# Inside one half-page step, VectorE's own product and sum go ahead of its sum of GpSimd's product

## The chip, the cores and the metric

The kernel runs on one core of a Trainium2 chip. The metric is the time of one launch on the device, in microseconds (us). Lower is better. The kernel before takes 874.13 us, the median of three runs (874.12 to 875.32).

## The reference

The reference is one inference step of a one-layer decoder trunk for 512 prompt tokens and 8 sample sequences (one new token each, 2048 past tokens in a paged cache). The part that matters here is the compression of the paged cache of the sample sequences. For each of the 8 sequences the cached rows are cut into segments of 16 tokens, and each segment is summed with two sets of 16 position weights. A compressed block is the first sum of one segment plus the second sum of the next:

```
def compress(rows, wpos, w, b):
    B, Tp = rows.shape[:2]
    seg = rows.reshape(B, Tp // CMP_STRIDE, CMP_STRIDE, NSA_KV_HEADS, HEAD_DIM)
    pooled = (jnp.einsum('bnjhd,jd->bnhd', seg[:, :-1], wpos[:CMP_STRIDE])
              + jnp.einsum('bnjhd,jd->bnhd', seg[:, 1:], wpos[CMP_STRIDE:]))
    return jnp.einsum('bnhd,de->bnhe', pooled, w) + b
```

Around it lie an input projection (`h @ w_in`), three kinds of attention, a matrix-memory recurrence, an output projection and a feed-forward network. Everything is float32.

## The kernel before

The values of the cache are compressed on VectorE and GpSimd; the keys are scored by TensorE straight from the pages. A sequence has 16 pages, loaded in two halves of 8 pages. There are 16 halves, numbered 0 to 15 here; half h belongs to sequence h // 2 and lives in one of two page buffers, h % 2. So "even" halves use one buffer and "odd" halves the other.

For each half h the engines do this:

- SyncE (`load_half`, L464) waits until the buffer is free: `comp_done` of half h - 2, and `slc_scored` of half h - 2 by TensorE. Then it issues 8 page loads (L471). Between two halves it issues one load of a weight slot (L455), which waits for GpSimd's `lo_ready`.
- GpSimd (`value_products`, L602) waits for the pages, and for `vmul_used` of half h - 1, and writes the product of the pages with the first 16 weights into the one scratch tile `tmpv`. Directly behind it stands the split of a weight slot (L622, the low part of a weight), which the projection on TensorE needs (`lo_ready`).
- VectorE (`half_sums`, L1474 on) waits for `vmul_ready`, sums `tmpv` over 16 (L1479, releases `tmpv` by `vmul_used`), multiplies the pages in place with the other 16 weights (L1482), and sums that (L1483, frees the page buffer by `comp_done`).
- After an odd half VectorE adds the two sums (L1630), and then, for sequences 1, 3, 4, 5 and 6, does one further piece of work for another branch: `gate_rows` (L1514 to L1518), `prompt_sums` (L1508, L1509, twice each), `gate_sums` (L1523 to L1525), `prompt_sums` again, and `gate_maxima` (L1529 to L1533). The last releases `rows_ready`, for which ScalarE waits before it evacuates the projection's item 17 (L1188).
- TensorE does one item of the projection (48 matmuls, L656) per half, between the scores of the pages (L740, L747). The item that stands behind half h needs the slot that GpSimd splits behind half h's product.

All engines run their instructions in the order of the program; nothing reorders them. The order is written out by hand.

Of the kernel before, what the change touches and what calls it, by code (L numbers as in the profile page):

```python
# [16 lines left out]
ALU = mybir.AluOpType  # L17
ACT = mybir.ActivationFunctionType
AX = mybir.AxisListType.X
# [148 lines left out]
def trunk_kernel(nc, xT, wst, par_d, con_d, hot_d, ltri_d, pt_d, cacheA, cacheV, winK, winV, mC, mst, plst, ffst,  # L168
                 o_y, o_fm, o_vn, o_st, o_snv, o_wk, o_wv, o_C, o_m, o_pool, o_sC, o_sn, o_sm, o_spool, o_ffp, o_ffs):
    with ExitStack() as ctx:  # L170
# [3 lines left out]
        def sem(name):  # L174
            return ctx.enter_context(nc.semaphore(name))
# [46 lines left out]
        def lay(at, parts):  # L222

            out = []
            for n in parts:
                out.append(arena[:, at:at + n])
                at += n
            return out


        qw, poolA, poolB, scs, _, sst = lay(0, [17 * P - 112, P, P, 2 * P, 256, 1024])
        scs = scs.rearrange("p (a n) -> p a n", a=2)
        poolA = poolA.rearrange("p (k n) -> p k n", k=2)
# [5 lines left out]
        tmpv = cst  # L239
# [90 lines left out]
        def par_(name, a=0, b=None, lo=0, hi=P):  # L330
            at, n = PAR[name]
            return par[lo:hi, at + a:at + (n if b is None else b)]
# [21 lines left out]
        vmul_ready, vmul_used = sem("vmul_ready"), sem("vmul_used")  # L354
# [1076 lines left out]
        def _(dve):  # L1431
            V = nc.vector
            chain = [0]

            def link(ins):

                chain[0] += 1
                ins.then_inc(dve_step, 1)
                dve.wait_ge(dve_step, chain[0])
# [34 lines left out]
            def half_sums(h):  # L1474


                b, s = h // 2, h % 2
                dve.wait_ge(vmul_ready, h + 1)
                V.tensor_reduce(poolA.rearrange("p k n -> p (k n)")[:, 64 * s:64 * s + 64], tmpv.rearrange("p (n j) -> p n j", j=16),  # L1479
                                AX, ALU.add).then_inc(vmul_used, 1)  # L1480
                v = pages[:, s, :, 2 * P:3 * P].rearrange("p a (n j) -> p a n j", j=16)
                link(V.tensor_tensor(v, v, par_("wpos", 48, 64).unsqueeze(1).unsqueeze(1).broadcast_to([P, HALF, 8, 16]), ALU.mult))  # L1482
                V.tensor_reduce(poolB.rearrange("p k n -> p (k n)")[:, 64 * s:64 * s + 64].rearrange("p (a n) -> p a n", a=HALF), v,  # L1483
                                AX, ALU.add).then_inc(comp_done, 1)
                dve.wait_ge(comp_done, h + 1)
                dve.wait_ge(vmul_used, h + 1)

# [127 lines left out]
            for c in range(1, 4):  # L1615
                group_mod(c)
                group_normed(c)
                if c == 2:
                    low(2)
            dve.wait_ge(rest_landed, 48)  # L1620
            half_sums(0)


            sample_query()
            for b in range(NB):
                for h in range(2 * b + (b == 0), 2 * b + 2):
                    half_sums(h)
                if b >= 2:
                    dve.wait_ge(blocks_done, b - 1)
                V.tensor_tensor(pooled[:, b % 2, 0:NCB], poolA.rearrange("p k n -> p (k n)")[:, 0:NCB],  # L1630
                                poolB.rearrange("p k n -> p (k n)")[:, 1:NCB + 1], ALU.add).then_inc(pooled_ready, 1)
                dve.wait_ge(pooled_ready, b + 1)
                if b == 1:
                    gate_rows()
                elif b == 3:
                    prompt_sums(0)
                elif b == 4:
                    gate_sums()
                elif b == 5:
                    prompt_sums(1)  # L1640
                elif b == 6:
                    gate_maxima()
# [373 lines left out]
            for m, (kind, t, _) in enumerate(PART2):  # L2016
# [15 lines left out]
                elif kind == "up":  # L2032
                    j, b = t % FC, t // FC
# [188 lines left out]
```

## Time and profile before

| what | us |
|---|---|
| median of three runs | 874.13 |
| the profiled execution, its own time | 879.95 |
| its span, first to last instruction | 877.3 |
| TensorE busy | 795.0 (91%) |
| VectorE busy | 499.2 (57%) |
| ScalarE busy | 328.9 (37%) |
| GpSimd busy | 297.0 (34%) |
| L602, GpSimd's product, 16 of them | 34.5 |
| L1479, VectorE's sum of it, 16 of them | 19.5 |
| L1482, VectorE's own product, 16 of them | 33.2 |

The profiled execution took 5.8 us more than the median of the runs. Its span is cut in 40 slices on the page; the halves fill slices 3 to 9 (46 to 206 us). Busy shares say little here: what counts is which wait ends last in that stretch.

### The profile page before, as it was taken

To read this page: it belongs to the slowest core of one execution; us is meant where nothing else is said; L and a number is where in the kernel's file an instruction comes from. 1 tells how busy PE (TensorE), PEld (TensorE's weight loads), DVE (VectorE), ACT (ScalarE), POOL (GpSimd) and SP (SyncE) were. 2 spreads that over 40 slices of the span, in tenths; PEclk is the share of its full clock that TensorE was granted. 3 is DMA by queue.
4 is the path that set the end of the run, shared out by engine and by line. 5 is a ranking of instruction groups with operands and counts; after the bars stand their busy time and mean duration, and the time that the engine had idled before them with its cause. 6 is when DMAs were issued, how large, how long until landed. Compare 5 with 4: busy or idle time off the path is not lost.

```text
span 877.3 us, 18760 instructions
## 1 busy us (share of the span) xinstructions
PE 795.0 (91%) x7525; PEld 727.1 (83%) x7525; DVE 499.2 (57%) x976; ACT 328.9 (37%) x601; POOL 297.0 (34%) x147
## 2 busy tenths in 40 slices
PE   2889999979998389998997999999999999999994
PEld 2888898878856256666996999999999999999993
DVE  3553767662256979875367566667211666666224
ACT  3332322423130146565334545554212445554221
POOL 0042664641000023345331344433443344433440
PEclk9699999999776669999999999999999999999997
DMA  9954878866249544413361233343223433322222
GB/s 348 324 200 125 266 237 258 275 210 213 92 130 377 136 117 120 116 57 108 129 262 49 85 100 119 120 119 86 97 96 105 113 108 110 96 97 76 95 67 97
DMA packets 72565, 130.17 MB, mean 148 GB/s; under 512 B 12621, under 2 KB 47325, under 8 KB 72225
## 3 DMA queue, kind: packets, MB, share of 16 engines
q1 hardware_dynamic: 66352, 113.27, 40.0%
q10 hardware_dynamic: 6096, 15.73, 5.7%
q8 instruction: 59, 0.97, 0.5%
q14 instruction: 26, 0.21, 0.1%
q0 software_dynamic: 32, 0.00, 0.0%
HBM read 123.52 MB, written 9.11 MB: 151 GB/s over the span
## 4 chain that ended last, share of the span: by engine, by line
PE 68%; DVE 15%; DMA 5%; SPq 3%; issue 3%; ACT 2%; POOL 2%; ACTq 0%; DVEq 0%; POOLq 0%
PE ps L656 51%; DMA arena<-cache_keys 3%; SPq L471 2%; PE ps L998 2%; PE ps L983 2%; PE ps L1020 2%; PE ps L1034 2%; DVE arena L1482 1%; POOL arena L602 1%; PE ps L674 1%; DMA arena<-weights 1%; DMA raw<-weights 1%; DVE arena L1483 1%; DVE arena L1479 1%; DVE arena L2043 1%
## 5 line engine op out<-in xcount | busy, mean ns | idle before, releaser
L656 PE MATMUL ps<-hR,wR 128*128 128x260 f32 x3456 | 431.1, 287 | 14.4 <-POOL wR L622 6.1
L656 PEld LDWEIGHTS ps<-hR,wR 128*128 128x128 f32 x3456 | 424.5, 191 | 19.1 <-issue 12.5
L622 POOL TENSOR_TENSOR wR<-raw,wR 128x1024 fp32r<-128x1024 f32 x92 | 221.6, 2410 | 294.8 <-ACT wR L1116 294.8
L1116 ACT ACTIVATE wR<-raw 128x1024 fp32r<-128x1024 f32 x94 | 99.4, 1057 | 213.5 <-PE ps L656 209.9
L656 PE MATMUL ps<-fR,wR 128*128 128x260 f32 x1056 | 128.1, 283 | 2.2 <-DVE fR L2014 2.0
L656 PEld LDWEIGHTS ps<-fR,wR 128*128 128x128 f32 x1056 | 127.0, 188 | 3.1 <-DVE fR L2014 2.4
L2038 DVE COPY arena<-arena 128x2 f32<-128x2 f32 x44 | 47.6, 1082 | 93.7 <-ACT arena L1408 93.7
L614 POOL TENSOR_SCALAR arena<-arena,fac 128x128 f32<-128x128 f32 (+3 forms) x32 | 40.4, 1265 | 163.4 <-DVE fac L1937 163.4
L602 POOL TENSOR_TENSOR arena<-arena,par 128x1024 f32<-128x1024 f32 x16 | 34.5, 2156 | 99.5 <-DMA arena<-cache_keys 94.4
L1999 DVE TENSOR_TENSOR t<-ps,mod 128x8 f32<-128x8 f32 x24 | 4.0, 166 | 108.5 <-PE ps L656 108.5
L1479 DVE TENSOR_REDUCE arena<-arena 128x64 f32<-128x1024 f32 x16 | 19.5, 1217 | 38.4 <-POOL arena L602 38.3
L1341 ACT ACTIVATE arena<-ps,nmx 128x128 f32<-128x128 f32 (+3 forms) x64 | 33.2, 525 | 19.8 <-DVE nmx L1928 19.8
L2043 DVE SCALAR_TENSOR_TENSOR arena<-arena,par 128x512 f32<-128x512 f32 x44 | 37.1, 844 | 1.6
L1408 ACT ACTIVATE arena<-arena,par 128x520 f32<-128x520 f32 x44 | 36.2, 824 | 1.5
L2042 DVE SCALAR_TENSOR_TENSOR arena<-arena,par 128x512 f32<-128x512 f32 x44 | 33.1, 752 | 1.6
L1482 DVE TENSOR_TENSOR arena<-arena,par 128x1024 f32<-128x1024 f32 x16 | 33.2, 2077 | 0.0
L1336 ACT ACTIVATE arena<-ps 128x256 f32<-128x256 f32 (+3 forms) x32 | 22.5, 704 | 26.1 <-PE ps L998 20.6
L998 PEld LDWEIGHTS ps<-con,arena 128*128 128x128 f32 x160 | 17.3, 143 | 17.5 <-issue 13.2
L983 PE MATMUL ps<-arena 64*128 64x128 f32 (+3 forms) x128 | 28.1, 516 | 2.3 <-DVE mod L1864 1.5
L1448 DVE TENSOR_TENSOR rstd<-rstd,sq 128x520 f32<-128x520 f32 x21 | 25.8, 1230 | 6.1 <-ACT sq L1099 5.1
L1405 ACT ACTIVATE arena<-ps 128x520 f32<-128x520 f32 x44 | 25.8, 587 | 6.7 <-DVE fR L2014 6.7
L998 PE MATMUL ps<-con,arena 128*128 128x128 f32 x160 | 25.2, 289 | 2.4 <-ACT arena L1336 1.2
(368 smaller groups left out, 840.9 us busy)
## 6 DMA issues: line engine op xcount, KB each, us to landing
raw<-weights SPq DMA_DIRECT2D x95, 512.0 KB, 3.7
arena<-cache_keys SPq DMA_DIRECT2D x128, 192.0 KB, 3.4
arena<-weights SPq DMA_DIRECT2D x27, 512.0 KB, 9.1
arena<-cache_values SPq DMA_DIRECT2D x128, 64.0 KB, 1.9
raw<-weights ACTq DMA_DIRECT2D x12, 512.0 KB, 6.6
arena<-weights ACTq DMA_DIRECT2D x9, 512.0 KB, 8.3
x<-xT SPq DMA_DIRECT2D x16, 260.0 KB, 4.2
out_y<-x SPq DMA_DIRECT2D x8, 260.0 KB, 2.2
```

What stands on the lines that cost most here:

```text
L602: nc.gpsimd.tensor_tensor(tmpv.rearrange("p (a n j) -> p a n j", a=HALF, j=16), pages[:, s, :, 2 * P:3 * P].rearrange("p a (n j) -> p a n ...
L614: nc.gpsimd.tensor_scalar(pr[v % 3][:, 1, 0:(b + 1) * P], pr[v % 3][:, 1, 0:(b + 1) * P], fac[:, v % 2, 1:2], None, ALU.mult)\
L622: nc.gpsimd.tensor_tensor(w_slot(i)[:, 1, :, :], raw[:, g % RAW, :, :], w_slot(i)[:, 0, :, :].bitcast(F32), ALU.subtract).then_inc(lo_read ...
L656: last = mm(ps[:, a + half, 0:TH], w_slot(i)[:, wp, k, :], src[:, hp, j, half * TH:(half + 1) * TH], start=(j == 0 and q == 0), stop=(j == ...
L983: last = mm(ps[:, 2 * (u % 2) + g, 0:n], pT[hr[g], hq, i * P:(i + 1) * P], pT[hr[g], t, 0:n], start=True, stop=True)
L998: last = nc.tensor.transpose(ps[:, 4 + g, c * P:(c + 1) * P], pr[u % 3][:, g, c * P:(c + 1) * P], ident)
L1116: A(w_slot(i)[:, 0, :, :], raw[:, g % RAW, :, :], ACT.Identity).then_inc(hi_ready, 1)
L1341: last = A(pr[k % 3][:, g, 0:n], ps[:, 2 * (k % 2) + g, 0:n], ACT.Exp, bias=nmx[:, k % 2, g:g + 1], accum_out=sm[:, k % 2, g:g + 1])
L1408: A(yab[:, b, :], zb[:, b, 2:T + 2], ACT.Identity, bias=par_("conv_b", t, t + 1), scale=par_("conv_w", 3 * t + 2, 3 * t + 3)).then_inc(y_r ...
L1482: link(V.tensor_tensor(v, v, par_("wpos", 48, 64).unsqueeze(1).unsqueeze(1).broadcast_to([P, HALF, 8, 16]), ALU.mult))
L2038: V.tensor_copy(ffo_p[:, t, :], z[:, S:S + 2])
L2043: last = V.scalar_tensor_tensor(y[:, 0:S], z[:, 0:S], w[0], y[:, 0:S], ALU.mult, ALU.add)
```

## The change

In `half_sums` the sum of GpSimd's product moves from the first place to the last. VectorE now starts with its own product and its own sum, whose end frees the page buffer (`comp_done`), and then sums `tmpv`, whose end frees the scratch tile (`vmul_used`). The wait for `vmul_ready` stays at the top, because the product overwrites the pages that GpSimd reads. No instruction is added or removed. The line numbers shift: the product is L1480 after the change, its sum L1481, and the sum of `tmpv` L1483.

```diff
                 dve.wait_ge(vmul_ready, h + 1)
-                V.tensor_reduce(poolA.rearrange("p k n -> p (k n)")[:, 64 * s:64 * s + 64], tmpv.rearrange("p (n j) -> p n j", j=16),
-                                AX, ALU.add).then_inc(vmul_used, 1)
                 v = pages[:, s, :, 2 * P:3 * P].rearrange("p a (n j) -> p a n j", j=16)
                 link(V.tensor_tensor(v, v, par_("wpos", 48, 64).unsqueeze(1).unsqueeze(1).broadcast_to([P, HALF, 8, 16]), ALU.mult))
                 V.tensor_reduce(poolB.rearrange("p k n -> p (k n)")[:, 64 * s:64 * s + 64].rearrange("p (a n) -> p a n", a=HALF), v,
                                 AX, ALU.add).then_inc(comp_done, 1)
+                V.tensor_reduce(poolA.rearrange("p k n -> p (k n)")[:, 64 * s:64 * s + 64], tmpv.rearrange("p (n j) -> p n j", j=16),
+                                AX, ALU.add).then_inc(vmul_used, 1)
                 dve.wait_ge(comp_done, h + 1)
                 dve.wait_ge(vmul_used, h + 1)
```

VectorE's queue before, halves 6 and 7 and the first `prompt_sums` behind them. `arena` holds the pages, `tmpv` and the sums; the tile written in L1508 and L1509 is scratch in `x`.

```order
L1479 TENSOR_REDUCE arena<-arena 128x64 [waits vmul_ready,pooled_ready]
L1482 TENSOR_TENSOR arena<-arena,par 128x8x128
L1483 TENSOR_REDUCE arena<-arena 128x64 [waits dve_step]
L1479 TENSOR_REDUCE arena<-arena 128x64 [waits vmul_ready,vmul_used,comp_done]
L1482 TENSOR_TENSOR arena<-arena,par 128x8x128
L1483 TENSOR_REDUCE arena<-arena 128x64 [waits dve_step]
L1630 TENSOR_TENSOR pooled<-arena 128x127 [waits blocks_done,vmul_used,comp_done]
L1508 TENSOR_TENSOR x<-arena,par 128x512 [waits evac_act,pooled_ready]
```

The same place after the change.

```order
L1480 TENSOR_TENSOR arena<-arena,par 128x8x128 [waits vmul_ready,pooled_ready]
L1481 TENSOR_REDUCE arena<-arena 128x64 [waits dve_step]
L1483 TENSOR_REDUCE arena<-arena 128x64
L1480 TENSOR_TENSOR arena<-arena,par 128x8x128 [waits vmul_ready,vmul_used,comp_done]
L1481 TENSOR_REDUCE arena<-arena 128x64 [waits dve_step]
L1483 TENSOR_REDUCE arena<-arena 128x64
L1630 TENSOR_TENSOR pooled<-arena 128x127 [waits blocks_done,vmul_used,comp_done]
L1508 TENSOR_TENSOR x<-arena,par 128x512 [waits evac_act,pooled_ready]
```

The product is now what stands first behind the wait for GpSimd, and the reduction of `tmpv` stands between `comp_done` and the next instruction.

## Rows read from the trace of the kernel before

**Rows 1.** The chain that ended last, shares of the span by line, of the page.
```profile
PE ps L656 51%; DMA arena<-cache_keys 3%; SPq L471 2%; PE ps L998 2%; PE ps L983 2%; PE ps L1020 2%; PE ps L1034 2%; DVE arena L1482 1%; POOL arena L602 1%; PE ps L674 1%; DMA arena<-weights 1%; DMA raw<-weights 1%; DVE arena L1483 1%; DVE arena L1479 1%; DVE arena L2043 1%
```

**Rows 2.** The chain in order of time, 121 to 140 us: start, length, what.
```profile
121.60 2.10 POOL arena L602
...
127.16 1.23 DVE arena L1483
...
132.93 5.11 DMA arena<-cache_keys
...
138.11 2.11 POOL arena L602
```

**Rows 3.** GpSimd's timeline, halves 6 and 7: start, length, instruction, idle before.
```profile
121.60 2.08 POOL L602 TENSOR_TENSOR arena<-arena,par 128x1024 f32<-128x1024 f32 x1 [6.52 <-DMA arena<-cache_keys]
123.64 2.40 POOL L622 TENSOR_TENSOR wR<-raw,wR 128x1024 fp32r<-128x1024 f32 x1
127.24 2.09 POOL L602 TENSOR_TENSOR arena<-arena,par 128x1024 f32<-128x1024 f32 x1 [1.20 <-DMA arena<-cache_keys]
129.29 2.39 POOL L622 TENSOR_TENSOR wR<-raw,wR 128x1024 fp32r<-128x1024 f32 x1
```

**Rows 4.** VectorE's timeline: half 6, behind half 7, and half 14.
```profile
123.78 1.22 DVE L1479 TENSOR_REDUCE arena<-arena 128x64 f32<-128x1024 f32 x1 [6.04 <-POOL arena L602]
124.92 2.20 DVE L1482 TENSOR_TENSOR arena<-arena,par 128x1024 f32<-128x1024 f32 x1
...
134.38 0.69 DVE L1508 TENSOR_TENSOR x<-arena,par 128x512 f32<-128x512 f32 x1
...
190.84 1.20 DVE L1482 TENSOR_TENSOR arena<-arena,par 128x1024 f32<-128x1024 f32 x1
```

**Rows 5.** TensorE's timeline, the items behind halves 6 and 7.
```profile
126.18 6.01 PE L656 MATMUL ps<-hR,wR 128*128 128x260 f32 x48 [0.63 <-POOL wR L622]
...
133.88 6.02 PE L656 MATMUL ps<-hR,wR 128*128 128x260 f32 x48
```

**Rows 6.** Timeline, VectorE and GpSimd starting close together, four places.
```profile
53.52 2.94 POOL L602 TENSOR_TENSOR arena<-arena,par 128x1024 f32<-128x1024 f32 x1 [5.12 <-DVE arena L1479]
...
90.32 2.38 POOL L622 TENSOR_TENSOR wR<-raw,wR 128x1024 fp32r<-128x1024 f32 x1 [1.17 <-ACT wR L1116]
90.38 3.40 DVE L1482 TENSOR_TENSOR arena<-arena,par 128x1024 f32<-128x1024 f32 x1
...
104.87 2.46 DVE L1518 SCALAR_TENSOR_TENSOR sq<-rstd 4x512 f32<-4x512 f32 x1
106.75 2.84 POOL L622 TENSOR_TENSOR wR<-raw,wR 128x1024 fp32r<-128x1024 f32 x1
...
436.76 2.40 POOL L622 TENSOR_TENSOR wR<-raw,wR 128x1024 fp32r<-128x1024 f32 x1 [3.36 <-ACT wR L1116]
436.80 2.92 DVE L1448 TENSOR_TENSOR rstd<-rstd,sq 128x520 f32<-128x520 f32 x1
```

**Rows 7.** Timeline of the further pieces on VectorE, and of ScalarE behind the last.
```profile
150.97 0.68 DVE L1523 SCALAR_TENSOR_TENSOR sq<-rstd,sq 4x512 f32<-4x512 f32 x1
...
186.96 2.19 DVE L1531 COPY x<-x 4x512 f32<-4x512 f32 x1
...
189.36 0.41 DVE L1533 TENSOR_SCALAR x<-x 4x512 f32<-4x512 f32 x1
...
189.87 0.60 ACT L1188 ACTIVATE sq<-ps 128x520 f32<-128x520 f32 x1 [13.45 <-DVE x L1533]
```

**Rows 8.** Timeline behind them, GpSimd and TensorE.
```profile
195.00 2.35 POOL L622 TENSOR_TENSOR wR<-raw,wR 128x1024 fp32r<-128x1024 f32 x1 [6.14 <-ACT wR L1116]
...
197.50 7.52 PE L656 MATMUL ps<-hR,wR 128*128 128x260 f32 x48 [2.76 <-POOL wR L622]
```

**Rows 9.** Busy by stretch: length, PE, PEld, DVE, ACT, POOL, clock, DMA share, GB/s.
```profile
129.31:145.83 16.52, 15.83 (x184) 14.57 (x184) 12.11 (x11) 4.46 (x10) 8.81 (x5) 1.00 0.79 259
...
178.62:197.00 18.38, 14.35 (x163) 12.29 (x162) 12.92 (x12) 4.35 (x10) 7.88 (x4) 0.91 0.65 207
```

## The prediction

> **What bounds the kernel now.** I read the page's chain first. TensorE's projections hold half of it, but the page loads, their issues and the lines of `half_sums` stand in it too [rows 1], so in that stretch something other than TensorE ends last. I then read the chain in order of time. From 90 to 187 us it is a ring, not a line: GpSimd's product, VectorE's three instructions, SyncE's issues, the landing, and GpSimd's product of the same buffer again [rows 2]. The reader is to see the period, 16.5 us for one pair of halves (121.60 to 138.11), and its longest part: from the end of the sum at 128.39 to the pages' landing at 138.04 it is 9.65 us for SyncE and the transfers. The table of stretches shows TensorE busy for 15.83 of 16.52 us with its clock at full [rows 9], so the ring is slower than TensorE by about 0.7 us a pair. TensorE's timeline shows that as a wait of 0.63 us for GpSimd's split L622 behind the even half, and none behind the odd half [rows 5]. Five such waits between 109 and 176 us add up to 3.4 us: that is the most that a shorter ring could give there.
>
> At the end of the stretch another chain takes over. VectorE's `gate_maxima` ends at 189.77, ScalarE had waited for it 13.45 us [rows 7], and through ScalarE's queue it holds the split L622 until 195.00 and TensorE's item until 197.50, where TensorE had idled 2.76 us [rows 8]. From `rows_ready` to that item it is 7.73 us of fixed work. So a microsecond later at `rows_ready` is a microsecond on the kernel.
>
> **What the timeline says of VectorE and GpSimd side by side.** The product L1482 takes 1.20 us alone, at 190.84, and 2.20 us in half 6 [rows 4]. In half 6 the split L622 ran from 123.64 to 126.04 [rows 3], and the product ended at 127.12, 1.08 us behind it. The same 1.08 us fit at 90.38: L622 ends at 92.70, the product at 93.78 [rows 6]. So the product does not run beside GpSimd's tensor_tensor; it starts when that ends. The other way round it is the same: L602 at 53.52 ran 2.94 us in place of 2.08, beside a product of VectorE that had started first [rows 6]. The reduction L1479, by contrast, takes its 1.22 us while L622 runs [rows 4].
>
> The Trainium skill says so in "SBUF — State Buffer", section "Who interferes with whom": a VectorE instruction with two SBUF inputs and a GpSimd instruction that reads SBUF exclude each other for the whole instruction, the first to issue wins, and tensor_reduce never contends. By that rule the reduction is just the instruction that costs nothing beside L622, and moving it away uncovers the product; the trace agrees by the 1.08 us.
>
> **The change part by part.** Call s the start of L602 of a half.
>
> 1. *When the page buffer comes free.* Before, L622 ends at s + 4.44, the product at s + 5.52 and its sum at s + 6.78 (121.60 to 128.38). The reduction L1479 lay under L622, so it was hidden. After the change the product is dispatched where L1479 was, 0.10 us behind L602's end, which is 0.14 us after L622 has started (123.78 against 123.64) [rows 3, 4]. Who wins? At 436.80 a tensor_tensor of VectorE started 0.04 us behind an L622 and lost: it took 2.92 us, and L622 its plain 2.40; five such places stand between 436 and 462 us. At 90.38 it was 0.06 us, and VectorE lost again [rows 6]. Only a VectorE instruction that was already waiting when L602 ended got in ahead of L622: L1518, waiting since 104.87, made L622 take 2.84 us [rows 6]. The product cannot wait already, since its semaphore comes from L602's end. So I take it that L622 wins: product to s + 5.52, sum to s + 6.78, `comp_done` as before. Gain 0. If VectorE won, `comp_done` would come at s + 4.64 (2.08 + 0.10 + 1.20 + 0.04 + 1.22), 2.1 us earlier. If product and reduction merely swapped places without any port, it would be 1.2 us earlier.
> 2. *When `tmpv` comes free.* Before at s + 3.40, while the next L602 came at s + 5.64 for its pages (127.24), so this was covered by the landing. After: s + 6.78 + 0.03 + 1.22 = s + 8.03, and with the 0.14 us from release to start (53.38 to 53.52) the next L602 comes at s + 8.16. The odd half's product moves 2.5 us back, its L622 ends at s + 12.6 in place of s + 10.08, and TensorE's odd item, at s + 12.28 before, starts 0.4 us late. That is inside the 0.63 us that TensorE waits behind the even half. Two halves of 8.16 us make 16.32, still under the ring's 16.5. Cost 0, with 0.2 us of cover left.
> 3. *What is queued on VectorE behind the odd half.* This is where the cover is gone. The sum L1630 ended at 134.34 and `prompt_sums` started at 134.38, that is s + 12.78 [rows 4], with GpSimd idle until 138.11. After, the odd half's third instruction ends at s + 16.2 and `prompt_sums` starts at about s + 16.5, exactly when the next even L602 starts. Its two L1508 have two SBUF inputs. By hand, with every close race to GpSimd: with a half-6 start at 121.0 (the first halves gain 0.6 us, since in half 2 L622 comes late and the product goes ahead of it), L1630 ends at 137.5, L602 of half 8 runs 137.5 to 139.6, the first L1508 ends at 140.2 and pushes L622 to 142.5, the second L1508 waits for that and ends at 143.0, its reduction at 143.7, the product at 145.0, the sum at 146.2. Before it was 144.90: +1.3 us on the ring. The next L602 of that buffer comes 9.7 us behind such a sum, and so on round the ring.
> 4. *`gate_sums` (2.65 us from 150.97 [rows 7]).* It meets L602 and L622 of half 10 in the same way, with three two-input instructions: its first ends at 158.6, the scan at 162.0, the third at 162.7, then product and sum at 165.1; before 161.42. +3.7 in all.
> 5. *`prompt_sums` again,* at half 12: sum at 183.35, before 177.68. +5.7 in all.
> 6. *`gate_maxima`.* One of its copies already met L602 before (2.19 us at 186.96 [rows 7]). After, L602 of half 14 runs 192.9 to 195.0, the scan starts behind it, and the last instruction ends at 197.6 against 189.77: +7.8. The 7.73 us behind it are unchanged.
> 7. *TensorE and SyncE.* TensorE's own items have up to 2 us of idle time a pair then, so they follow. The slot loads between the halves wait for L622, which for odd halves comes later, but before the next `comp_done`; 0. After half 15 the reduction adds 1.25 us on VectorE, under the item that TensorE still runs; 0.
>
> The sum is +7.8 us with all races to GpSimd. In steps 3 and 5 the races are within 0.05 us; going to VectorE, step 3 costs 0.4 instead of 1.3. If half of such items fall that way I get about +6. I take +7.0. Against the profiled execution: 879.95 + 7.0 = 886.95. It took 5.8 us more than the median, so for the runs I take 874.13 + 7.0 = 881.1 us. This case's own range: +3 us (each piece 0.4 to 1 us) to +11 us: 877 to 885.
>
> A bound from below for steps 3 to 6 is 0, if the pieces run wholly in gaps of GpSimd; from above, each of the four pieces shifts the ring by its full length and both of GpSimd's instructions, some 3 us each, 12 us.
>
> **The rivals.**
>
> *A. VectorE wins the port; faster.* The place is the 0.14 us between L622's start and the product's. GpSimd's recorded starts may not be where it takes the port: back to back, L622 is shown starting 0.04 us before L602 ends [rows 3]. If the product is in by then, `comp_done` comes 2.1 us earlier, the ring falls to 14.4 us, and TensorE with 15.8 us binds. The five waits go: 3.4 us. L622 would end at s + 5.6, which TensorE can bear, since its items lag. `gate_maxima` comes 3.4 us earlier less the 1.2 us of the reduction before L1630, so the item at 197.50 gains 2 to 3.4 us. About 871.2 us. It decides from the product's start within L602's end, not behind it. For it: the case of L1518. Against it: six starts in which VectorE was 0.04 to 0.06 us late and lost.
>
> The skill's "Perfetto Trace Analysis", section "GPSIMD Engine Instruction", warns that a GpSimd instruction's span is unreliable and should be read by spacing from start to start. That is the reason why A is not ruled out; the spacing here, 2.04 us for L602, does not decide it.
>
> *B. No measurable change.* `comp_done` is where it was (step 1), the odd half moves inside its cover (step 2), and the pieces of VectorE fall into gaps, at a price that the 0.6 us of the first halves and TensorE's 0.63 us per pair absorb. What stays is half 13: L1630 later by some 1 to 2 us, of which the copy's wait of 1.7 us gives a part back. 874 to 876: 875 us. Against it: step 3's start coincides with L602 to 0.1 us.
>
> *C. TensorE's clock as well.* Before 197.50 TensorE had idled 2.76 us, and that item took 7.52 us in place of 6.01 [rows 5, 8]; the granted clock of 178.62 to 197 us is 0.91, a mix of the full 2.4 GHz and the 1.2 GHz level, against 1.00 in the pairs before [rows 9]. Idle times of about 2 us a pair would come earlier. Each would cost 1.5 us of TensorE, mostly in its slack; two or three on the path add 3 to 4 us: 885 us and above.
>
> **How the numbers follow.** Forecast 0.60, C 0.12, A 0.15, B 0.13. What a measurement of this kernel tells from no change is about 0.2%, 1.75 us. A lies below 872.4, B within for the most part, the forecast and C above. Faster 0.15, same 0.12, slower 0.73. The range leaves out A and the top of C: 873.5 to 886. For the slower cases alone, which hold 0.72, it is 877 to 886.
>
> **What would show it.** In the profile of the changed kernel L1480 should take about 3.3 us on average (2.40 - 0.14 + 1.08), not 1.2; if it takes 1.2 and L622 3.5, A is right. L602 of odd halves should wait for VectorE and start 8.2 us behind the even one. L1508 and L1523 to L1525 should be lengthened by GpSimd. L1533 should end near 196 to 198, and the item of TensorE behind it start 7.7 us later. The forecast is wrong if L1533 ends before 191, or if the time from that item to the end is not what it was.

## The result: slower by 0.9%, and the profile after

| | before | after |
|---|---|---|
| median of six runs | 874.85 us | 883.56 us |
| lowest to highest | 874.12 to 878.28 | 881.68 to 885.40 |
| ratio, 95% interval | | 1.009 (1.0063 to 1.0116) |
| the profiled execution, its span | 879.95, 877.3 | 884.57, 882.8 |

The forecast was 881.1 us, slower. The two profiled executions differ by 4.6 us only, less than the medians. TensorE's item 7 starts at 93.01 in the one of before and at 91.08 after, and only 0.75 us of these 1.9 lie ahead of the first half (its product starts at 46.33 and 45.58). Over all eleven profiles of this case item 7 starts between 87.1 and 93.3 us. In the five with the order of before it starts at 90.8 to 93.3, in the six with the new order at 87.1 to 92.5. Whether the new order gains something there stays open. I compare from item 7 on, start to start, so what lies ahead of it is left out.

GpSimd's timeline of the changed kernel, halves 6 to 9, answers to [rows 3].

```profile
118.86 2.15 POOL L602 TENSOR_TENSOR arena<-arena,par 128x1024 f32<-128x1024 f32 x1 [3.65 <-DMA arena<-cache_keys]
120.97 2.40 POOL L622 TENSOR_TENSOR wR<-raw,wR 128x1024 fp32r<-128x1024 f32 x1
127.32 2.10 POOL L602 TENSOR_TENSOR arena<-arena,par 128x1024 f32<-128x1024 f32 x1 [3.95 <-DMA arena<-cache_keys]
129.37 2.40 POOL L622 TENSOR_TENSOR wR<-raw,wR 128x1024 fp32r<-128x1024 f32 x1
135.38 2.20 POOL L602 TENSOR_TENSOR arena<-arena,par 128x1024 f32<-128x1024 f32 x1 [3.61 <-DVE arena L1483]
137.53 2.84 POOL L622 TENSOR_TENSOR wR<-raw,wR 128x1024 fp32r<-128x1024 f32 x1
145.43 2.09 POOL L602 TENSOR_TENSOR arena<-arena,par 128x1024 f32<-128x1024 f32 x1 [5.06 <-DVE arena L1483]
```

VectorE's timeline beside it answers to [rows 4]: half 6, then the first prompt_sums and half 8.

```profile
121.12 3.34 DVE L1480 TENSOR_TENSOR arena<-arena,par 128x1024 f32<-128x1024 f32 x1 [2.06 <-POOL arena L602]
124.49 1.22 DVE L1481 TENSOR_REDUCE arena<-arena 128x64 f32<-128x1024 f32 x1
125.63 1.21 DVE L1483 TENSOR_REDUCE arena<-arena 128x64 f32<-128x1024 f32 x1
...
135.65 2.47 DVE L1508 TENSOR_TENSOR x<-arena,par 128x512 f32<-128x512 f32 x1
138.16 0.69 DVE L1509 TENSOR_REDUCE x<-x 128x32 f32<-128x512 f32 x1
138.88 2.05 DVE L1508 TENSOR_TENSOR x<-arena,par 128x512 f32<-128x512 f32 x1
140.96 0.69 DVE L1509 TENSOR_REDUCE x<-x 128x32 f32<-128x512 f32 x1
141.68 1.22 DVE L1480 TENSOR_TENSOR arena<-arena,par 128x1024 f32<-128x1024 f32 x1
142.94 1.22 DVE L1481 TENSOR_REDUCE arena<-arena 128x64 f32<-128x1024 f32 x1
```

In half 6 the product is dispatched 0.15 us behind L622 and takes 3.34 us. Its sum ends at 125.71, 6.85 us behind L602's start; before it was 6.78 us. The page buffer comes free no earlier. Behind half 7, from 135.65 on, both L1508 take over 2 us in place of 0.69: the first ends 0.54 us behind L602, the second 0.56 us behind L622 (140.37), which the first has itself pushed to 2.84 us. That is step 3 of the prediction in its own rows.

The table of stretches, one row for each pair of halves from half 6 on (start of L602 to start of L602). Columns as in [rows 9]. First the kernel before:

```profile
121.60:138.11 16.51, 15.88 (x185) 14.63 (x184) 12.12 (x11) 5.36 (x13) 8.88 (x4) 1.00 0.80 257
138.11:154.65 16.54, 15.85 (x184) 14.57 (x184) 11.94 (x10) 4.80 (x11) 8.89 (x5) 1.00 0.77 246
154.65:170.90 16.25, 15.54 (x182) 14.26 (x181) 11.68 (x11) 5.04 (x12) 8.87 (x5) 1.00 0.83 277
170.90:186.66 15.76, 15.31 (x180) 14.05 (x180) 11.41 (x10) 4.08 (x6) 8.87 (x4) 1.00 0.81 255
```

Then the changed kernel:

```profile
118.86:135.38 16.52, 15.98 (x184) 14.56 (x183) 11.59 (x8) 5.50 (x13) 8.97 (x5) 1.00 0.82 265
135.38:153.45 18.07, 16.06 (x185) 14.62 (x184) 15.37 (x12) 4.73 (x11) 9.40 (x5) 1.00 0.74 230
153.45:172.03 18.58, 16.06 (x177) 14.62 (x176) 15.89 (x11) 5.62 (x11) 9.40 (x4) 0.94 0.74 237
172.03:190.89 18.86, 18.29 (x198) 16.91 (x198) 16.14 (x13) 3.29 (x5) 9.38 (x4) 0.97 0.72 227
```

The first pair, with no further piece of VectorE before it, is as long as before: 16.52 against 16.51. The three pairs that begin with such a piece are longer by 1.5, 2.3 and 3.1 us, 7.0 us together. VectorE's busy time in them rises by 3.4 to 4.7 us, but these rows do not hold the same instructions (12, 11 and 13 against 10, 11 and 10): a further piece that fell into the end of one pair before falls into the start of the next one now. Instruction by instruction it is clearer. The two L1508 behind half 7 take 4.52 us in place of 1.38, those behind half 11 4.50 in place of 1.38, and `gate_sums` 6.44 us in place of 2.57. Over the whole kernel VectorE has 976 instructions as before, and is shown busy for 511.4 us in place of 499.2: the difference, 12.2 us net, is time in which it stood before the port.

VectorE's release of `rows_ready`, ScalarE and TensorE at the end of the stretch answer to [rows 7, 8].

```profile
194.63 0.41 DVE L1533 TENSOR_SCALAR x<-x 4x512 f32<-4x512 f32 x1
...
195.14 0.60 ACT L1188 ACTIVATE sq<-ps 128x520 f32<-128x520 f32 x1 [15.62 <-DVE x L1533]
...
202.76 7.49 PE L656 MATMUL ps<-hR,wR 128*128 128x260 f32 x48 [2.95 <-POOL wR L622]
```

From ScalarE's start to item 19 (202.76) it is 7.6 us, as before. The stretch is bounded by TensorE's items 7 and 20. Before:

```profile
93.01 6.03 PE L656 MATMUL ps<-hR,wR 128*128 128x260 f32 x48
...
207.24 5.98 PE L656 MATMUL ps<-hR,wR 128*128 128x260 f32 x48
```

After:

```profile
91.08 6.04 PE L656 MATMUL ps<-hR,wR 128*128 128x260 f32 x48
...
212.51 6.02 PE L656 MATMUL ps<-hR,wR 128*128 128x260 f32 x48
```

From start to start that is 121.43 us, before 114.23: +7.2. Of these, 5.4 us lie between items 7 and 18, where the ring is, and 1.8 us between items 18 and 19, where `rows_ready` is waited for. From item 20 to the end of the span it is 670.3 us, before 670.1. Behind item 7 the loss lies in this stretch alone.

The waits between 80 and 215 us, longest in total (who waited for whom, us, times, longest), show the new owner of the scratch tile's wait:

```profile
POOL arena L602 <- DVE arena L1483: 34.8, 8, 5.6
DVE arena L1480 <- POOL arena L602: 34.3, 9, 7.9
POOL arena L602 <- DMA arena<-cache_keys: 20.4, 5, 5.9
```

Before, GpSimd's product waited 50.2 us, 13 times, for the pages, and never for VectorE in this part. Now 8 of its 13 waits are for VectorE's late sum.

### The profile page after: what moved, and what is told of

The parts are those of the page before. It is cut to its first block, busy times and chain, and to the rows that moved or that the text cites. A ratio compares the mean times of both kernels' runs of the same rounds, so it can differ in the third digit from the quotient of the medians.

```text
span 882.8 us, 18760 instructions
## 1 busy us (share of the span) xinstructions
PE 794.2 (90%) x7525; PEld 726.3 (82%) x7525; DVE 511.4 (58%) x976; ACT 328.7 (37%) x601; POOL 298.0 (34%) x147
## 4 chain that ended last, share of the span: by engine, by line
PE 62%; DVE 11%; issue 3%; ACT 2%; DMA 1%; POOL 1%; SPq 1%; ACTq 0%; DVEq 0%; POOLq 0%
PE ps L656 47%; PE ps L998 2%; PE ps L983 2%; PE ps L1020 2%; PE ps L1034 2%; DMA raw<-weights 1%; DVE arena L2043 1%; PE ps L844 1%; DVE sq L1461 1%; PE ps L877 1%; DVE x L2065 1%; PE ps L1017 1%; DVE x L1508 1%; DMA arena<-cache_keys 0%; PE ps L821 0%
## 5 line engine op out<-in xcount | busy, mean ns | idle before, releaser
L622 POOL TENSOR_TENSOR wR<-raw,wR 128x1024 fp32r<-128x1024 f32 x92 | 222.5, 2420 | 295.7 <-ACT wR L1116 295.7
L602 POOL TENSOR_TENSOR arena<-arena,par 128x1024 f32<-128x1024 f32 x16 | 34.6, 2165 | 102.8 <-DMA arena<-cache_keys 68.0
L1480 DVE TENSOR_TENSOR arena<-arena,par 128x1024 f32<-128x1024 f32 x16 | 36.0, 2253 | 36.5 <-POOL arena L602 36.4
L1928 DVE TENSOR_REDUCE nmx<-ps 128x2 f32<-128x256 f32 (+3 forms) x32 | 26.4, 825 | 1.1
```

The source lines that it names most:

```text
L602: nc.gpsimd.tensor_tensor(tmpv.rearrange("p (a n j) -> p a n j", a=HALF, j=16), pages[:, s, :, 2 * P:3 * P].rearrange("p a (n j) -> p a n ...
L622: nc.gpsimd.tensor_tensor(w_slot(i)[:, 1, :, :], raw[:, g % RAW, :, :], w_slot(i)[:, 0, :, :].bitcast(F32), ALU.subtract).then_inc(lo_read ...
```

## The experiments

All ratios are to the kernel before on the same chip. The column "items 7 to 20" is from each run's one profiled execution.

| run | median us | ratio, 95% interval | items 7 to 20, us |
|---|---|---|---|
| before | | | 114.2 |
| after | 883.56 | 1.009 (1.0063 to 1.0116) | 121.4 |
| e1_product_first | 869.79 | 0.9942 (0.9914 to 0.9971) | 106.1 |
| e2_two_scratch | 876.53 | 1.0009 (0.9984 to 1.0034) | 115.9 |
| e3_sums_late | 879.20 | 1.0041 (1.0018 to 1.0065) | 118.3 |
| e4_sums_late_in_before | 874.85 | 0.9992 (0.9963 to 1.0021) | 111.5 |
| e5_maxima_early_in_before | 867.61 | 0.9885 (0.9852 to 0.9918) | 108.0 |
| e6_split_waits_in_before | 878.05 | 1.0019 (0.9998 to 1.0040) | 114.9 |
| e7_product_first_maxima_early | 865.12 | 0.9878 (0.9842 to 0.9913) | 104.4 |
| e8_after_again | 881.22 (one) | | 121.0 |
| e9_before_again | 874.97 (one) | | 110.2 |

**e1_product_first** adds one wait to the changed kernel:

```diff
+                if 7 <= i < N_IN:
+                    pool.wait_ge(prod_done, half)
                 pool.wait_ge(hi_ready, i + 1)
```

(`prod_done` is counted up by VectorE's product.)

> The changed kernel, with one wait added on GpSimd: from half 2 on, the split L622 behind a half's product waits until VectorE's own product of that half has ended, so VectorE has the port first. Theory (the split takes the port 0.14 us ahead of VectorE's product and covers it for 2.3 us): the product takes 1.2 us instead of 3.3, the page buffer comes free at s + 4.6 instead of s + 6.8 (s: start of GpSimd's product of the half), the ring falls under TensorE's 15.8 us a pair, and the kernel takes 870 to 873 us, faster than both. Rival (the loss comes from the release of the scratch tile and the length of VectorE's queue, the port has no part): the added wait only delays the split and with it TensorE's item; 883 us or more.

Measured: ratio 0.9942, 1.5% under the changed kernel's. Half 6 in its timeline, GpSimd and VectorE (the lines are shifted: L603 the product on GpSimd, L625 the split, L1483 VectorE's product, L1485 its sum, L1487 the sum of `tmpv`):

```profile
118.29 2.08 POOL L603 TENSOR_TENSOR arena<-arena,par 128x1024 f32<-128x1024 f32 x1 [2.55 <-DMA arena<-cache_keys]
120.48 1.23 DVE L1483 TENSOR_TENSOR arena<-arena,par 128x1024 f32<-128x1024 f32 x1 [4.44 <-POOL arena L603]
121.74 1.22 DVE L1485 TENSOR_REDUCE arena<-arena 128x64 f32<-128x1024 f32 x1
121.78 2.40 POOL L625 TENSOR_TENSOR wR<-raw,wR 128x1024 fp32r<-128x1024 f32 x1 [1.41 <-DVE arena L1483]
122.87 1.21 DVE L1487 TENSOR_REDUCE arena<-arena 128x64 f32<-128x1024 f32 x1
```

The product takes 1.23 us, and its sum ends at 122.96, 4.67 us behind L603's start, 2.2 us earlier than in the changed kernel. The split now lies beside the two reductions, and loses nothing by them: 2.40 us. The next even half starts 14.71 us on, in place of 16.52, and TensorE does not wait for a split in it. The order of the change is an improvement as soon as the port is given to it; without that it is a loss. This settles the port, and it is rival A of the prediction brought about by force. Against the first profile of the kernel before, the stretch is 8.1 us shorter: 2.7 us between items 7 and 18, and 5.5 us behind item 18, where `gate_maxima` comes earlier and item 19 takes 6.00 us in place of 7.52. The median, 869.79 us, lies just under the 870 to 873 expected.

**e6_split_waits_in_before** puts the same wait into the kernel before, with the sum of `tmpv` still first.

> The kernel before, sum of GpSimd's product first as it was, with only the wait of e1_product_first: the split behind a half's product waits until VectorE's own product has ended. Theory: the product goes from s + 3.3 to s + 4.5 without a wait, the page buffer comes free at s + 5.8 (1 us earlier than before, 1.2 us later than in e1), the split ends at s + 7.0, 1.4 us later than in e1 and 2.5 us later than before. The ring falls to 15.5 us, below TensorE's 15.8, but the even item of TensorE began at s + 4.6 and now waits for the split: it slips once by some 2 us, not per pair. 873 to 876 us, so that e1's gain needs both the order and the port. Rival (the port alone makes the gain, the order has no part): 869 to 871 us.

Measured: 1.0019 (0.9998 to 1.0040), no gain. VectorE and GpSimd in half 6 (L1482 the sum of `tmpv`, L1485 the product, L1487 its sum):

```profile
120.05 1.22 DVE L1482 TENSOR_REDUCE arena<-arena 128x64 f32<-128x1024 f32 x1 [3.42 <-POOL arena L603]
121.19 1.22 DVE L1485 TENSOR_TENSOR arena<-arena,par 128x1024 f32<-128x1024 f32 x1
122.44 1.22 DVE L1487 TENSOR_REDUCE arena<-arena 128x64 f32<-128x1024 f32 x1
...
122.48 2.40 POOL L625 TENSOR_TENSOR wR<-raw,wR 128x1024 fp32r<-128x1024 f32 x1 [2.54 <-DVE arena L1485]
```

The product is short here too, but GpSimd idles 2.54 us in front of the split instead of 1.41. TensorE waits 0.28 us for the split of half 6 and 0.95 to 1.31 us for those of halves 8, 10 and 12, before 0.45 to 0.71 us. So the port alone gives nothing that can be measured; order and port together do. The four kernels stand beside each other: neither, 1; order alone, 1.009; port alone, 1.0019; both, 0.9942.

**e2_two_scratch** gives the changed kernel a second scratch tile, in a part of `x` that is free then:

```diff
-        tmpv = cst
+        tmpv = [cst, md]
...
-                if h:
-                    pool.wait_ge(vmul_used, h)
-                nc.gpsimd.tensor_tensor(tmpv.rearrange("p (a n j) -> p a n j", a=HALF, j=16),
+                if h == 1:
+                    pool.wait_ge(h_lo, KD)
+                if h >= 2:
+                    pool.wait_ge(vmul_used, h - 1)
+                nc.gpsimd.tensor_tensor(tmpv[h % 2].rearrange("p (a n j) -> p a n j", a=HALF, j=16),
```

(The sum reads `tmpv[s]` likewise. The wait for `h_lo` at half 1 is new too.)

> The changed kernel with two scratch tiles for GpSimd's product (even and odd halves), so that the late sum of it holds back no product. Theory: the odd half goes back to s + 5.6, the pieces of VectorE behind it start about s + 14.0 (before s + 12.8), ahead of GpSimd's next product at s + 16.5, and do not meet it; the page buffer comes free as before at s + 6.8, so nothing is gained either: 874 to 877 us. Rival (the page buffer itself is freed later by the new order, or VectorE's queue is simply too long): 880 to 884 us, as the changed kernel.

Measured: 1.0009 (0.9984 to 1.0034), so the loss is gone within what can be told. All of GpSimd's products from half 2 on but the last wait for the pages again, and the last for nothing. The expectation that the pieces would not meet GpSimd was wrong: the first L1510 (L1508 before the shift) took 2.75 us in it, a product of GpSimd 2.52. So the loss goes although collisions stay. That the earlier start of the odd half makes the difference is argued from this, and no run shows it by itself.

**e3_sums_late** and **e4_sums_late_in_before** move both prompt_sums behind the loop, in the changed kernel and in the one before:

```diff
-                elif b == 3:
-                    prompt_sums(0)
...
-                elif b == 5:
-                    prompt_sums(1)
...
+            for kv in range(2):
+                prompt_sums(kv)
+
             dve.wait_ge(blocks_done, NB)
```

> The changed kernel with both prompt_sums moved from behind sequences 3 and 5 to behind the loop, where VectorE idles 8.8 us. Theory (each of the pieces behind an odd half meets GpSimd's product and split of the next even half and delays the ring): the two pieces' share goes, some 3 to 4.5 us: 879 to 880.5 us; what is left is gate_sums and gate_maxima. Rival (the pieces play no part, the loss is spread over all halves): 883 us.

> The kernel before with both prompt_sums moved behind the loop in the same way. Theory: there they lay in a gap of GpSimd and off the ring, so nothing is gained: 873.5 to 875 us. Rival (they cost the ring in the kernel before too, so that their cost is no part of the difference): 870 to 872 us.

Measured: 1.0041 and 0.9992. In the changed kernel the two pieces account for about half of the loss (0.9% to 0.4%; the two intervals just touch, so the share is rough); in the kernel before they cost nothing that can be measured. The same work has a price only where the new order puts it. The profile of e4 shows a stretch of 111.5 us, 2.7 less than that of before, but its median does not; e9 below says how little one profile is worth at that size.

**e5_maxima_early_in_before** swaps two pieces of the kernel before: gate_maxima behind sequence 5, the second prompt_sums behind sequence 6.

```diff
                 elif b == 5:
-                    prompt_sums(1)
-                elif b == 6:
                     gate_maxima()
+                elif b == 6:
+                    prompt_sums(1)
```

> The kernel before with gate_maxima one sequence earlier (behind sequence 5) and the second prompt_sums one later (behind sequence 6). Theory (at the end of the stretch rows_ready, not the ring, holds ScalarE, the split and TensorE's item 19, which had idled 1.8 and 2.8 us there): rows_ready comes some 15 us earlier, the idle time of 4.5 us and the slower item of 7.5 us go, and 3 to 5 us are gained: 869.5 to 871.5 us. Rival (the last pages would hold the same item anyway): 874 to 875 us.

Measured: 0.9885 (0.9852 to 0.9918), about 10 us of 876.6; I had expected 3 to 5. TensorE's items 18 and 19:

```profile
183.49 6.01 PE L656 MATMUL ps<-hR,wR 128*128 128x260 f32 x48
...
192.21 6.03 PE L656 MATMUL ps<-hR,wR 128*128 128x260 f32 x48
```

They are 8.7 us apart in place of 14.3, and the second takes 6.03 us in place of 7.52: the mechanism is right. Between items 7 and 20 that gives 6.2 us against the first profile of the kernel before, but only 2.2 us against its second (e9 below). Another 2.7 us lie behind item 20 in this profile. They are no evidence for the swap: behind item 20 the eleven profiles take 666.6 to 672.3 us, and e3 and e4, which leave `gate_maxima` where it was, take 666.6 and 666.7. So the time shows the gain of about 10 us, and the profiles trace only a part of it.

**e7_product_first_maxima_early** joins e1 and e5.

> e1_product_first with gate_maxima behind sequence 5 and the second prompt_sums behind sequence 6. Theory: the two gains are of different places (the ring, and the wait for rows_ready behind it) and add up in part: the idle time of TensorE before item 19 goes too, 866 to 868 us. Rival (one hides the other, TensorE is the bound at its 15.8 us a pair and the last pages come no earlier): 869 to 870 us.

Measured: 0.9878 (0.9842 to 0.9913), 865.12 us, the fastest median. Its stretch, 104.4 us, is 3.6 us under e5's in one profile each, but the ratio is not told apart from e5's 0.9885. That the two gains add up is not shown by the times.

**e8_after_again** and **e9_before_again** are second looks at the two kernels.

> The changed kernel as it is, a second profiled execution, to see how far one profile can be trusted. Theory (the order of port and queue sets the stretch, not chance): from TensorE's item 7 to its item 20 (start to start) it takes 120 to 123 us again (121.4 in the first), and eight products take 3.3 us. Rival (the 7.2 us over the kernel before in that stretch are the luck of one execution): it falls between 114 and 118 us.

> The kernel before as it is, a second profiled execution. Theory: the stretch from item 7 to item 20 takes 113 to 115 us again (114.2 in the first). Rival (the stretch varies from one execution to the next as much as the change moved it): 110 or less, or 117 or more.

Measured: 121.0 and 110.2 us. The changed kernel repeats to 0.4 us, and eight products take 3.26 to 3.34 us again. The kernel before does not repeat: I had expected 113 to 115, and 110.2 is at the rival's bound of 110. One difference is `gate_maxima`:

```profile
184.91 0.42 DVE L1531 COPY x<-x 4x512 f32<-4x512 f32 x1
...
186.74 2.08 POOL L602 TENSOR_TENSOR arena<-arena,par 128x1024 f32<-128x1024 f32 x1 [6.48 <-DMA arena<-cache_keys]
```

It has ended at 185.95, ahead of L602 of half 14, so its copy takes 0.42 us in place of 2.19. That is 1.8 of the 4.0 us; the rest lies earlier in the stretch and was not traced. The cost of the change in this stretch is thus 7 to 11 us, not just 7.2. Over the whole span the two pairs of profiles differ by 5.5 and 4.8 us, since the changed kernel reached item 7 earlier in both, by 1.9 and 6.2 us; the medians say 8.7. That the ring of VectorE and GpSimd ties the meetings together in the changed kernel, and slack lets them come and go in the one before, is a reading of two profiles each.

## Why the prediction was right

- *Bound by the ring and by rows_ready.* Right. The ring's period sets the pairs, and e5 shows the second chain by itself. Its size is not settled: e5 gives 6.2 us in the stretch against the first profile of before (4.5 us of idle time, and 1.5 us for the slow item of 7.52 us) and 2.2 us against the second.
- *Step 1, GpSimd keeps the port.* Right. In 8 of 16 halves the product takes 3.25 to 3.34 us; in the others VectorE comes late enough, or the split does, and it takes 1.2. I had written "about 3.3 us on average", and the average is 2.25: I had left out the halves behind a further piece, and the first three. `comp_done` came at s + 6.85 against s + 6.78 forecast.
- *Step 2, the odd half moves to s + 8.16 inside its cover.* Measured 8.46 in half 7 (127.32 less 118.86); it waited for its pages and not for VectorE. The pages of the odd half came later than I had assumed, and the pair was 16.52 us all the same: cost 0, as forecast. In e8 half 7 did wait for VectorE, at s + 8.15. In the pairs that begin with a further piece the odd product comes 10.0 to 10.6 us behind the even one, which the 8.2 us of "what would show it" did not allow for. But the cover of 0.2 us at the even half was none: L602 of half 8 waited for VectorE and started at s + 16.52.
- *Steps 3 to 5, the further pieces meet GpSimd.* Right, with sizes 0.1 to 0.7 us too large. The forecasts are on the profile's own clock; set against item 7, the sum of half 8 ends 1.2 us later than before (forecast 1.3), that of half 10 3.2 us (3.7), that of half 12 5.0 us (5.7).
- *Step 6, rows_ready.* Forecast +7.8, measured +7.2 (103.96 against 96.76 us behind item 7's start). The meeting went another way than forecast: the scan was already running (190.35) when L602 of half 14 started (190.89). L602 took 2.54 us, and the next instruction of VectorE (L1530) 2.37 in place of 0.68. L1533 ended at 195.04, just ahead of the 196 to 198 given as a sign; item 7 had started 1.9 us earlier.
- *Step 7, SyncE and TensorE follow.* Right. TensorE idled 2.04 us before item 16 and then took 7.49 us for it; the granted clock was 0.77 over the item and 0.94 over that pair, a mix of the 1.2 and 2.4 GHz levels. So what rival C names did occur, but inside the slack that the ring left: in e8 item 16 took 6.01 us, and the stretch was 121.0 us against 121.4.
- *The size.* +7.0 was forecast, 8.7 measured. The nearness is in part luck. The +7.0 stands between +7.8, with all races to GpSimd, and about +6, with half of them to VectorE. Every close race between product and split went to GpSimd, so the case of +7.8 came about, and it gave +7.2 in the profile. The sum was also made against one execution of the kernel before, in which `gate_maxima` met GpSimd (2.19 us for a copy). In e9 it did not. A term that "already met L602 before" was counted as unchanged, where in other executions it is new. What makes up the 1.7 us between 7.0 and 8.7 is not shown.

Rival A (VectorE wins the port) did not occur by itself, and e1 shows what it was worth: 0.6%, about 5 us under the kernel before, against some 3 us forecast. Its estimate had no term for the slow item 19, which takes 1.5 us less in e1. Rival B fell with step 3.

## What to carry to other kernels

A reduction that stands behind another engine's work may be there for its place and not for its result: ask of each instruction what it can lie beside, before moving one that cannot. Where two engines share a port and one gets its release from the other's instruction, the engine that had its next instruction queued behind it won every time here; give the port by a semaphore where it is worth more. And where a queue is moved back by 2.5 us, what counts is not the cover of the moved instruction but of all that stands behind it.

## What the runs showed of the hardware

- VectorE's product started 0.15 to 0.18 us behind GpSimd's split in eight halves of the changed kernel, and GpSimd had the port every time; the loser waited for the whole instruction. The Trainium skill has this rule in "SBUF — State Buffer", section "Who interferes with whom": the first to issue holds the shared pair for the whole instruction. The trace agrees: in all eight the product ended 1.08 to 1.09 us behind L622.
- A scan with two inputs stands before the port too. `gate_sums` in the changed kernel:

```profile
153.72 2.46 DVE L1523 SCALAR_TENSOR_TENSOR sq<-rstd,sq 4x512 f32<-4x512 f32 x1
156.22 3.30 DVE L1524 TENSOR_TENSOR_SCAN rstd<-sq 4x512 f32<-4x512 f32 x1
159.55 0.68 DVE L1525 TENSOR_TENSOR x<-x,rstd 4x512 f32<-4x512 f32 x1
```

The scan on four partitions takes 1.21 us alone (151.69 before) and 3.30 us here, where it ends 1.08 us behind L622 (155.60 to 158.44). That is as far behind the split as the product on 128 partitions ends, so a narrow instruction waits too.
